# A new order from the state space outputs to the attention units, four score buffers, and filler products at the norms

## The reference, cut to what matters

```
h = x + W_out(concat[rms(S5), rms(conv), rms(NSA)] * g)   # three head groups read one projection of RMSNorm(x)
h = h + CrossAttn(RMSNorm(h), RMSNorm(mem))               # 4 heads, 256 memory tokens
h = h + FFN(RMSNorm(h))       # layer 0: dense SwiGLU of 2816; layer 1: top 2 of 8 experts of 2816
```

## Time and profile before

| | us |
|---|---|
| median of 3 runs | 1404.94 (1403.8 to 1406.1) |
| the profiled execution | 1405.65 |
| its span, from first to last instruction | 1403.8 |
| TensorE busy | 1304.5 (93%) |
| DVE busy | 641.7 (46%) |
| ACT busy | 419.4 (30%) |
| POOL busy | 90.8 (6%) |
| mean granted TensorE clock | 0.957 |

### The profile page before, as it was taken

The page is one execution under the profiler, slowest core; times in us unless marked ns, Lnnn a source line. Parts: engine busy times, 40 slices in busy tenths (PEclk is TensorE's granted clock), DMA queues, the critical chain, the costliest instruction groups (busy, mean ns, idle before and its releaser), DMA issues.

```text
span 1403.8 us, 48116 instructions
## 1 busy us (share of the span) xinstructions
PE 1304.5 (93%) x21350; PEld 1071.8 (76%) x21350; DVE 641.7 (46%) x1405; ACT 419.4 (30%) x831; POOL 90.8 (6%) x139
## 2 busy tenths in 40 slices
PE   6987897999999898879868999999999999999997
PEld 4754545777777585445548999999999999999996
DVE  6866512102422227463235555554555555455554
ACT  4424412100102112242222333333333333333332
POOL 0450000000000017100100000000000000000000
PEclk9997899899999999879978999999999999999999
DMA  8430042243341053100657999999999999999980
GB/s 358 192 121 1 2 167 112 95 180 146 124 180 60 34 234 150 61 2 0 242 227 284 428 426 426 426 427 426 426 426 426 426 426 426 426 427 426 426 367 32
DMA packets 32576, 357.66 MB, mean 255 GB/s; under 512 B 3683, under 2 KB 5347, under 8 KB 6412
## 3 DMA queue, kind: packets, MB, share of 16 engines
q1 hardware_dynamic: 30368, 353.78, 60.8%
q10 hardware_dynamic: 2156, 3.18, 0.7%
HBM read 355.88 MB, written 1.06 MB: 254 GB/s over the span
## 4 chain that ended last, share of the span: by engine, by line
PE 89%; DVE 4%; ACT 3%; issue 2%; POOL 1%; DMA 0%; DVEq 0%; ACTq 0%; POOLq 0%
PE bank L2031 28%; PE bank L1510 28%; PE bank L2047 14%; PE bank L1980 5%; PE bank L1518 2%; PE bank L2093 2%; PE bank L2018 2%; PE bank L1530 1%; PE bank L1771 1%; PE bank L1650 1%; PE bank L1833 1%; ACT ring L566 1%; PE bank L1581 0%; DVE ring L943 0%; POOL rs L845 0%
## 5 line engine op out<-in xcount | busy, mean ns | idle before, releaser
L2031 PE MATMUL bank<-R,ring 128*64 128x80 f32 x11264 | 421.7, 233 | 0.7 <-DVEq L925 0.7
L2031 PEld LDWEIGHTS bank<-R,ring 128*64 128x64 f32 x11264 | 403.1, 137 | 8.4 <-issue 8.4
L1510 PE MATMUL bank<-ring 128*128 128x256 f32 (+1 forms) x1408 | 377.1, 427 | 18.6 <-ACT ring L654 5.6
L1510 PEld LDWEIGHTS bank<-ring 128*128 128x128 f32 x1408 | 272.7, 195 | 122.5 <-issue 80.0
L816 ACT ACTIVATE ring<-ring 128x1024 f32<-128x1024 f32 x176 | 186.0, 1057 | 146.6 <-PE bank L2047 146.6
L2047 PE MATMUL bank<-zz,ring 128*64 128x80 f32 x5632 | 224.8, 233 | 0.0
L2047 PEld LDWEIGHTS bank<-zz,ring 128*64 128x64 f32 x5632 | 207.9, 137 | 0.0
L1472 DVE SCALAR_TENSOR_TENSOR zz<-zz,bank 128x80 f32<-128x80 f32 x176 | 41.9, 238 | 198.7 <-PE bank L2031 198.2
L1451 DVE COPY ring<-ring 128x1024 f32<-128x1024 f32 x177 | 121.6, 687 | 1.9 <-DVE R L1441 1.9
L1455 DVE COPY ring<-ring 128x1024 f32<-128x1024 f32 x177 | 121.5, 687 | 0.2
L812 ACT ACTIVATE X<-bank 128x80 f32<-128x80 f32 x176 | 41.8, 238 | 247.2 <-PE bank L2031 247.2
(11 more groups left out here) (295 smaller groups left out, 1016.8 us busy)
## 6 DMA issues: line engine op xcount, KB each, us to landing
ring<-moe_w_dram SPq DMA_DIRECT2D x177, 1536.0 KB, 11.1
ring<-ffn_w_dram SPq DMA_DIRECT2D x11, 3072.0 KB, 10.0
ring<-w_in_dram SPq DMA_DIRECT2D x6, 2048.0 KB, 10.2
ring<-w_out_dram SPq DMA_DIRECT2D x4, 2048.0 KB, 8.5
ring<-w_x_dram SPq DMA_DIRECT2D x2, 3072.0 KB, 10.5
ring<-w_small_dram SPq DMA_DIRECT2D x2, 2896.0 KB, 9.6
ring<-w_in_dram SPq DMA_DIRECT2D x2, 2144.0 KB, 20.3
ring<-bias_rows_dram ACTq DMA_DIRECT2D x1, 1536.0 KB, 9.1
```

Of the source, the lines that this page charges most:

```text
L1510: i = pe.matmul(out_ap, a, b, start=(k == 0), stop=(k == n - 1))
L2031: e = pe.matmul(pb[out_bank][c0:c0 + 64, 0:CAP], half[:, P * k + c0:P * k + c0 + 64], xg[:, k], start=(k == 0), stop=(k == KT - 1), tile_p ...
```

## The change

Five things, in both layers unless said otherwise:

1. ACT copies the convolution's output (L654) right after the squares of the queries, before the compressed keys.
2. TensorE's order up to the first scores becomes: `kv_tile(1)`, `ys(1)`, gate logits, query turns, key turns, `cmp1`, `scores(0)`, convolution turn, `glu`, `scores(1)`, loop. On DVE the gelu of the state outputs comes before the norms of the keys. `cmp2` and DVE's and ACT's parts of the compression, of the gate output and of the LayerNorm move into the loop, as functions called at units 1 to 5. Some banks change with the order.
3. Score buffers, maxima and turned buffers are four each: two in `scr` as before, two in the space of `xT`, which the projections no longer need. Unit `v` uses buffer `(v + 2) % 4` and waits for the turn of unit `v - 4`.
4. `scores((v + 3) // 2)` is issued after odd `v`, at the end of the iteration; it was `scores(v // 2 + 1)` after even `v`, right behind the turn. The constants move most of the inserted work by some units.
5. `keep_warm(name, n)`: n products of the unit matrix with 256 columns of constants, into a bank that nobody reads. Seven before the turns of the norms of mix 1, ffn 0 and ffn 1, three before the count of the experts' tokens, four before the first gathers.

```diff
-C_SCORES, C_EXPS, C_TURN, C_VALUES = (1, 10), (2, 11), (3, 12), (5, 14)
-CONV_TURN, CONV_GAIN, CONV_TANH, CONV_SILU, CONV_OUT, CONV_COPY = 6, 7, 7, 8, 9, 10
-COMBINE, Y_SQUARES, Y_SCALE = 9, 11, 14
+C_SCORES, C_EXPS, C_TURN, C_SUMS, C_VALUES = (4, 12), (5, 13), (6, 14), (7, 15), (8, 15)
+CONV_TURN, CONV_GAIN, CONV_TANH, CONV_SILU, CONV_OUT, CONV_COPY = 8, 9, 9, 10, 10, 11
+COMBINE, Y_SQUARES, Y_SCALE = 9, 12, 15
...
+        if l:
+            a("warm_mix", 3, 0)
...
-        a("cmp1_", 1)
         a("qT0_", 5); a("qT1_", 0)
-        a("kT_", 6)
+        a("kT_", 6); a("cmp1_", 7)
+        a("cvT", 2); a("cmp2v", 2)
         a("glu0_", 3, 2); a("glu1_", 4, 2)
-        a("cmp2_", 7, 2); a("cvT", 2); a("cmp2v", 2)
-        a("cmpT", 3)
+        a("cmp2_", 3, 2); a("cmpT", 3)
...
+        a("warm_ffn", 3, 0)
...
-            add("count", 3)
+            add("warm_count", 0, 0); add("count", 3); add("warm_pick", 1, 0)
...
-        nmx = sb("nmx", [P, 2, 2])
+        nmx = sb("nmx", [P, 4, 2])
...
+        spare = xT[:].rearrange("p k t -> p (k t)").rearrange("p (b s) -> p b s", b=4)
+        s_of = [scr[:, 0], scr[:, 1], spare[:, 0], spare[:, 1]]
+        pt_of = [scr[:, 2], scr[:, 3], spare[:, 2], spare[:, 3]]
+
+        def at(v): return (v + 2) % 4
...
                     act.activation(sq[:], ps(f"q{i}_{l}")[:], ACT.Square).then_inc(banks.drain(f"q{i}_{l}"), 1)
+                nm = f"conv{l}"
+                banks.wait(act, nm)
+                for a in range(2):
+                    k = act.activation(ca[:, a], ps(nm)[:, 256 * a:256 * a + 256], ACT.Identity, scale=0.5,
+                                       bias=par[:, G_CB + 2 * l + a:G_CB + 2 * l + a + 1])
+                k.then_inc(banks.drain(nm), 1)
                 banks.wait(act, f"kvc{l}")
...
                     if v < 2 * NH:
                         act.wait_ge(sem["max_ready"], u + 1)
                         for b in range(2):
-                            e = probs(u, b, scr[:, u % 2, b * nk:b * nk + nk], 1.0, sums[:, i, b, hh:hh + 1])
+                            e = probs(at(v), b, s_of[at(v)][:, b * nk:b * nk + nk], 1.0, sums[:, i, b, hh:hh + 1])
                         e.then_inc(sem["probs_ready"], 1)
+                    if v == 1:
+                        cmp_tanh()
+                        for g in range(NT):
+                            glu_tanh(g)
                     if v:
                         pi, ph = divmod(v - 1, NH)
-                        pt_copy(u - 1, f"pT{pi}{ph}_{l}", 2 * P * (pi + 1))
+                        pt_copy(at(v - 1), u - 4, f"pT{pi}{ph}_{l}", 2 * P * (pi + 1))
+                    if v == 2:
+                        cmp_squares()
+                    if v == 3:
+                        ln_squares()
...
-                    if u >= 2:
+                    if v >= 4:
+                        banks.wait(dve, transposed(u - 4))
+                    elif u >= 2 and v < 2:
                         banks.wait(dve, transposed(u - 2))
...
-                    if v == 0:
+                    if v == 1:
+                        cmp_inner()
+                        ln_center()
+                        glu_out()
+                        cmp_gated()
+                    if v == 2:
+                        cmp_sums()
+                    if v == 3:
                         cmp_keys()
-                    if v == 1:
+                    if v == 4:
                         cmp_keys_in()
-                    if v == 3:
+                    if v == 5:
+                        ln_scale()
+                    if v == 6:
...
                     if v in C_EXPS:
                         c_scores(C_EXPS.index(v))
-                    if v in C_TURN:
-                        c_sums(C_TURN.index(v))
+                    if v in C_SUMS:
+                        c_sums(C_SUMS.index(v))
...
+            def keep_warm(name, n):
+
+                banks.open(pe, name)
+                for _ in range(n):
+                    e = pe.matmul(ps(name)[:, 0:256], ident, cst[:, 0:256], start=True, stop=True)
+                done(name, e)
...
+                if l:
+                    keep_warm(f"warm_mix{l}", 7)
                 turn_tiles("mix_T", l, xn, wait_norm(NORM[f"mix{l}"]))
...
-                               conv, lambda: kvc_half(0), lambda: kvc_half(1), lambda: kv_tile(0), lambda: kv_tile(1), gate_logits]
+                               conv, lambda: kvc_half(0), lambda: kvc_half(1), lambda: kv_tile(0), lambda: kv_tile(1), lambda: ys(1), gate_logits]
...
+                def conv_turn():
+                    nm = f"cvT{l}"
                     banks.open(pe, nm)
+                    drained(f"conv{l}")
...
+                def glu():
+                    pe.wait_ge(sem["ys_g"], l + 1)
...
+                def cmp2():
+                    banks.open(pe, f"cmp2v{l}")
+                    banks.open(pe, f"cmp2_{l}")
+                    pe.wait_ge(sem["cmp_g"], l + 1)
...
                 scores(0)
+                conv_turn()
+                glu()
+                scores(1)
                 for v in range(2 * NH):
...
-                    if v % 2 == 0 and v + 2 < 2 * NH:
-                        scores(v // 2 + 1)
-                    if v == 0:
+                    if v == 3:
                         cmp_turn()
                     if v:
                         values(v - 1)
+                    if v == 1:
+                        cmp2()
...
+                    if v % 2 and v + 3 < 2 * NH:
+                        scores((v + 3) // 2)
...
+                keep_warm(f"warm_ffn{l}", 7)
                 turn_tiles("ffn_T", l, xn, wait_norm(NORM[f"ffn{l}"]))
...
+            keep_warm("warm_count", 3)
             nm = "count"
...
+            keep_warm("warm_pick", 4)
             HALVES = (0, 64)
```

More of the change, by code:

```diff
@@ L690, in _, with cmp_squares @@
                        .then_inc(banks.drain(nm), 1)
[L692 to L695, removed]
+                def cmp_squares():
+                    banks.wait(act, f"cmp2_{l}")
+                    act.wait_ge(sem["head_sum"], 7 * l + 4)
+                    act.activation(sq[0:NCMP, 0:128], ps(f"cmp2_{l}")[0:NCMP, 0:128], ACT.Square, scale=0.5)\
+                       .then_inc(banks.drain(f"cmp2_{l}"), 1)
                 def mem_values(i, src, nm):
@@ L1149, in _ @@
                 gelu_inner(w, y).then_inc(sem["ys_w"], 1)
+                for i in range(NT):
+                    dve.wait_ge(sem["k_rs"], 2 * l + i + 1)
+                    c = c_qk(l, i)
+                    kv = ps(f"kv{i}_{l}")[:].rearrange("p (b c e d) -> p b c e d", b=2, c=2, e=2)
+                    dve.tensor_tensor(kn[:, i].rearrange("p b (e d) -> p b e d", e=2), kv[:, :, 0],
+                                      spread(rs[:, c + 8:c + 12].rearrange("p (b e) -> p b e", b=2), [P, 2, 2, HD]), ALU.mult)\
+                       .then_inc(banks.drain(f"kv{i}_{l}"), 1)
                 dve.wait_ge(sem["ys_t"], l + 1)
@@ new lines, in ln_center @@
+                def ln_center():
+                    nm = f"cvT{l}"
+                    banks.wait(dve, nm)
+                    pv = ps(nm)[:].rearrange("p (i c) -> p i c", i=NT)
+                    own(dve.tensor_reduce(rs[:, 140:142], pv, AX, ALU.add))
+                    own(dve.tensor_scalar(rs[:, 142:144], rs[:, 140:142], -1.0 / CW, None, ALU.mult))
+                    own(dve.tensor_tensor(lnb[:], pv, spread(rs[:, 142:144], [P, NT, CW]), ALU.add))
+                    signal(banks.drain(nm))
+                    signal(sem["ln_centered"])
@@ new lines, in cmp_gated, with glu_out @@
+                def cmp_gated():
+                    dve.wait_ge(sem["cmp_t"], l + 1)
+                    dve.scalar_tensor_tensor(cmpx[:, 3], cmpx[:, 2], 1.0, cmpx[:, 0], ALU.add, ALU.mult).then_inc(sem["cmp_g"], 1)
+                def glu_out():
+                    for i in range(NT):
+                        nm = f"glu{i}_{l}"
+                        dve.wait_ge(banks.drain(nm), banks.count(nm, None, False) + 1)
+                        banks.wait(dve, f"qT1_{l}")
+                        dve.scalar_tensor_tensor(xn[:, i, 0:CW], scr[:, 3, 256 * i:256 * i + 256], 1.0, ps(nm)[:, 0:256],
+                                                 ALU.add, ALU.mult).then_inc(banks.drain(nm), 1)
@@ L1698, in _ @@
                     done(nm, e)
-                ys(1)
-                nm = f"cvT{l}"
-                banks.open(pe, nm)
-                drained(f"conv{l}")
-                for i in range(NT):
-                    for a in range(2):
-                        e = pe.transpose(ps(nm)[:, 256 * i + P * a:256 * i + P * a + P], ca[:, a, P * i:P * i + P], ident)
-                done(nm, e)
-                for i in range(NT):
-                    drained(f"kv{i}_{l}", 3)
-                nm = f"kT_{l}"
@@ L1710, in _ @@
-                banks.open(pe, nm)
-                for b in range(2):
-                    for i in range(NT):
```

(15 more changed lines are left out.)

162 lines of the change are left out of this document (73 added, 89 removed).

## The result

The changed kernel took 1389.16 us (median of four runs, 1387.6 to 1391.4), the kernel before 1404.87 beside it: ratio 0.9886, 95% interval 0.9872 to 0.9899. That is 1.1% faster, clear of the noise, inside the range, and 6 us above the forecast of 1383. The profiled execution, the slowest of the four, took 1391.4 us with a span of 1389.6, 14.2 less than before.

The account below looks back on a forecast made before the run. From about 750 us TensorE and the DMA rings are full, so only an earlier start shortens the expert stage. Gains 4.0 + 6.6 + 3.0 + 3.2 + 5.5 = 22.3 us gave a forecast of 1383 us, range 1366 to 1395.

Parts of the forecast that it names:

- Part 1: Key/value projection: the convolution copy moved ahead removes kv_tile(0)'s waits; gain 1.85 us in layer 0, 5.4 in layer 1.
- Part 2: Projection's end to first turn: the new order takes 13.6 us at full clock; gain 8.2 and 7.2 us.
- Part 3: Unit loop with four buffers and moved scores: 55 us, 6.0 longer in each layer, -12.0 together.
- Part 4: Fillers at the norms keep the clock up: gain 3.0 at ffn 0, 3.2 at mix 1, 5.5 at ffn 1.
- three pauses: Unit loop: TensorE idles 4.2, 7 and 2.6 us; half clock afterwards adds 2 to 3 us each.
- a third pause: Late in the unit loop, before turn 14: TensorE waits 2.6 us for DVE's compressed scores and unit 14.
- the pause of "4.2 us" after unit 5: Unit loop: TensorE, done with unit 4, stands 4.2 us before scores(4) until DVE drains unit 7.
- The full-clock layout of 49.8: Unit loop: queues laid out from the rows' durations at full clock for layer 0 come to 49.8 us.
- the buffers hide little, and the earlier start pays: Attention: loops lengthen 6.0 us a layer, yet earlier starts leave a net gain of 4.0 and 6.6 us.
- the count's three would cost 2.6: Experts' token count: if the clock were already low, its three fillers would cost 2.6 us and delay it 0.4.
- the 6.4 us that full clock promised: ffn 1 to gathers: full clock saves 1.2 at turns, 1.8 router, 1.1 count, 2.3 gathers; 5.5 was taken.
- moved with its start, as said: Expert stage: still 659 us from its first product to the end, so an earlier start arrives whole.

Follow-up runs that it names:

- The shorter lead: Changed kernel with VectorE waiting for the turn of the unit two back, not four, so only two score buffers are used: 1390.30 us.
- fillers everywhere: Changed kernel plus fillers in the unit loops, cross attention and ahead of the router, and the experts' constants loaded ahead of the last norm: 1364.48 us.
- The copy alone: Kernel before with only ACT's convolution copy moved ahead of the compressed keys' copies: 1396.57 us.
- the fillers alone: Kernel before with only the five filler groups at the norms, the count and the gathers: 1394.94 us.
- old order, all fillers: Old order, two buffers, early copy, fillers at norms, gate product, loop, cross attention and router, experts' constants loaded early; timed beside the kernel before: 1374.31 us.
- half the fillers: The kernel of 1364.5 us with about half the fillers in every group (7 to 3, 8 to 4): 1381.01 us.

## Why the prediction was near, and where it was off

The mechanism was right in parts 1 and 2, at the first two norms of part 4, and in the sign of part 3. Mis-sized were the loops, by 4.4 us together, and the way from ffn 1 to the experts, by 1.8. The gain of the profiled executions in us, step by step (minus is a loss); the sum of the last column is 14.2.

| step | forecast | trace |
|---|---|---|
| Part 1, kv_tile(0)'s waits and clock | 7.25 | 7.5 |
| Part 2, to the first turn | 8.2 + 7.2 | 8.4 + 7.4 |
| Part 3, the loops | -12.0 | -8.1 - 8.3 |
| Part 4, ffn 0, mix 1 | 3.0 + 3.2 | 3.0 + 3.2 |
| Part 4, ffn 1 to the experts | 5.5 | 3.7 |
| the start, not in the sum | 0 | -1.4 |
| between the steps and in the expert stage | 0 | -1.2 |

**Part 1** held. No wait is left in either layer. In layer 1 the stretch from the FFN's end to the projection's end went from 85.95 to 77.09 us (479.20 to 556.29); 3.2 of the 8.9 are the norm's and 5.7 this wait's.

**Part 2** held: 13.35 us in both layers for 13.6 laid out, at full clock in every slice.

**Part 3 had the right sign and the wrong size.** "Half clock in what follows adds 2 to 3 us each: 56. I take 55": it was 57.1 and 57.5. By the forecast's own terms three pauses add 6 to 9 us to 49.8, which is 56 to 59; I took the lower end and then 1 less, for a third pause that might miss. It did not miss, and a fourth pause came first. I had laid out that the compressed sums hold unit 3 and that scores(2) go at 109.3, and passed over it: the three pauses that I priced were the later ones. TensorE stood 1.63 us there, and the clock stayed at half from 109.6 to 130.0, in layer 1 from 573.8 to 590.9 (worked out from the slices at either end). In half clock TensorE was late itself, so the pause of "4.2 us" after unit 5 shrank to 0.36 and 0.92, but the clock was low there already. The combine stood 3.54 and later 0.66 and 0.63 us (7 forecast), turn 14 2.05 (2.6).

The full-clock layout of 49.8 was too long, not too short: the loop measured 46.7 with 27 fillers in it. The low clock costs 10.4 us in the loop, where I had 5 to 6. So two errors stand against each other, 3 us too much layout and 5 too little for the clock, and that the forecast of the loop missed by only 2.1 and 2.5 us is in part luck.

So the forecast's last inference, "the buffers hide little, and the earlier start pays", is half shown. The shorter lead, which leaves two buffers in use, cost 1.1 us in the changed kernel, no more than the runs scatter. The earlier start pays 15.8 before the turns, and the loops take 16.4 back. With fillers everywhere, order and buffers pay 9.8, and 7.3 if only the layer is counted twice in which both ran at full clock. There the loop is longer by 2.3 in the new order for a start that comes 6 earlier (mix turn to first turn 86.5 against 92.5).

**Part 4** was right at ffn 0 and mix 1. At ffn 1 I had the fall ahead of the gathers; it came in the router, two steps earlier. Count kept its 2.27 us, the fillers took 2.93 and 3.76 at half clock, the case for which I had said "the count's three would cost 2.6". The gathers had the clock back halfway, 2.71. The experts' constants made VectorE 0.6 us late, but the slow fillers alone would have held the count as long: VectorE's selection ended at 720.66, they at 720.8. So of the 6.4 us that full clock promised, the turns gave their 1.2 and the gathers' stretch 1.8 of 2.3, but router and count together 0.6 of 2.9. With three fillers ahead of the router and the load moved, first norm turn to first expert product (the experts' first product at 730.24 and 703.48) went from 18.5 to 16.6 us.

I had set a rule of the Trainium skill (TensorE: Matmul & The Clock Gate, What's actually happening) against the trace, that the clock falls only after a stretch idle as a whole. The trace of the changed kernel does not agree with that rule either: the clock fell in a slice in which TensorE worked 2.00 of 2 us, 1.5 us after a pause of 0.98 (0.79 of a 2 us slice leaves 0.84 us at half, from 717.2; the router began at 715.7). By the rule ffn 1 would have given 6.4 us; it gave 3.7.

**The start.** The first state inputs took 1.4 us longer in the profiled execution. No instruction there was changed. In the twelve experiments the turns behind them begin at 26.86 to 28.36 us in the old order and at 27.38 to 28.63 in the new. The two ranges overlap, so chance is the likelier reading, though three of the five old-order kernels are ahead of all seven new ones; it is not shown.

**The expert stage** moved with its start, as said: 659.4 us from its first product against 658.7.

**Open.** The copy alone (9.2) and the fillers alone (10.8) sum to 20.0 and together give 16.1. The profiled execution of the two together is 1385.6, which is the sum; the other three lie at 1389 to 1391. Their mean granted clocks are 0.969 to 0.971, against 0.974 in the profiled one, and the slowest has the lowest: the difference goes with how long the clock was low. Where it fell in those three is open, since none of them has a trace.

## What to carry to other kernels

Price a reordering twice, at the clock that the old trace shows and at the full one, and price every pause of TensorE in it, also the first: here order and buffers were worth 7 to 10 us with the clock held, nothing that could be told from zero with fillers at the norms alone, and a loss of 4.8 without fillers. Fill pauses of TensorE with idle products into a bank that is drained and about to be used; they need no wait that the next product into that bank hasn't. In the new order they gave 12.2 us at the norms and 24.7 more in the pauses of the loops, the cross attention and the router (the constants' load included), where new order and buffers alone gave none; with half of them 16.5 of these 36.8 were lost again.

## What the runs showed of the hardware

The clock fell at the end of an idle stretch of 1.63 us (changed kernel, both layers), 1.1 us behind one of 1.71 (old order, all fillers, layer 0), behind one of 2.60 (half the fillers, ffn 0), 0.8 and 1.8 us behind one of only 1.00 (half the fillers, ahead of scores(2)), and once inside the router's products. It held through 1.71 in layer 1 of that same old-order kernel, through 1.89 us ahead of the gathers (all fillers), and through 2.60 at ffn 1 and 2.68 at mix 1 (half the fillers). So no single length of pause tells the two apart in these runs. The windows in which it fell behind the 1.00 us, in layers 0 and 1 (columns of the earlier trace rows):

```profile
110.00:112.00 2.00, 2.00 (x21) 1.61 (x23) 1.43 (x5) 1.97 (x10) 0.39 (x2) 0.69 0.00 0
568.00:570.00 2.00, 2.00 (x16) 1.23 (x17) 0.84 (x3) 1.97 (x10) 0.05 (x1) 0.53 0.00 0
```

Once down it stayed so for 20 us in the loop (109.6 to 130.0), in which TensorE had no pause above 0.92 us; behind the ffn 0 norm of the kernel before it was back in the slice at 256, within 9 us of the first turn at 248.09.

At the kernel's start TensorE issued its products at about half the later rate, though the granted clock reads 1.00. These are windows of the changed kernel:

```profile
22.00:24.00 2.00, 2.00 (x6) 1.60 (x5) 1.80 (x7) 1.96 (x2) 0.34 (x3) 1.00 0.99 426
...
26.00:28.00 2.00, 2.00 (x11) 1.77 (x10) 1.97 (x2) 0.00 (x0) 0.00 (x0) 1.00 0.98 410
```

Both are busy throughout, with the same products over 256 columns, 6 in one and 11 in the other. In the kernel before, the window from 22 to 24 us already has 11, which fits the 1.4 us that its profiled execution is ahead at the start. Whether the reading is wrong there or something else holds the products is not shown.
